# Opening of a first attention: doubled keys counted apart, maxima between the value block's tiles, values taken in two halves, last queries rounded later

## What is computed

```python
def attention_mixer(h, w_qkv, q_g, k_g, w_o, rope):   # 16 query heads, 4 key/value heads, head width 64
    qkv = h @ w_qkv
    q, k, v = jnp.split(qkv, [1024, 1280], axis=-1)
    q = rmsnorm(q.reshape(B, S, 16, 64), q_g)
    k = rmsnorm(k.reshape(B, S, 4, 64), k_g)
    v = v.reshape(B, S, 4, 64)
    q = axial_rope(q, rope)
    k = axial_rope(k, rope)
    # for each block of queries
    s = jnp.einsum('bqhgd,bkhd->bhgqk', qblk, k) * scale
    p = jax.nn.softmax(s, axis=-1)
    o = jnp.einsum('bhgqk,bkhd->bqhgd', p, v)
    return o @ w_o
```

## Time and profile before

| | |
|---|---|
| time, median of 3 runs | 1970.55 us (1969.24 to 1971.86) |
| time of the profiled execution | 1969.77 us |
| its span | 1968.0 us |
| TensorE busy | 1940.5 us, 99% of the span |
| VectorE, ScalarE, GpSimd busy | 1096.2, 751.2, 590.7 us |
| mean granted TensorE clock | 0.995 of full speed |

### The profile page before, as it was taken

How to read it: one execution, slowest core, us unless ns; L and a number is a source line. 1 busy time by engine, 2 the same in 40 slices (tenths; PEclk the granted TensorE clock), 3 DMA queues, 4 the chain that set the end, 5 groups by cost and what they waited for, 6 DMA issues and landing times.

```text
span 1968.0 us, 23603 instructions
## 1 busy us (share of the span) xinstructions
PE 1940.5 (99%) x9254; PEld 1601.6 (81%) x9254; DVE 1096.2 (56%) x1086; ACT 751.2 (38%) x838; POOL 590.7 (30%) x528
## 2 busy tenths in 40 slices
PE   9899999999999999999999999999999999999998
PEld 7655788888887988888888887889888888888886
DVE  6754355555557547455455557874344474545456
ACT  6456332222235534332232235455552353222223
POOL 1201279997000001289996002523210100000000
PEclk9999999999999999999999999999999999999999
DMA  6411244443322221144443233412133312323221
GB/s 230 108 10 22 86 150 171 152 159 111 107 86 97 92 102 43 65 167 154 171 149 123 86 106 113 118 43 74 55 107 107 107 51 78 107 85 107 87 105 64
DMA packets 42763, 204.51 MB, mean 104 GB/s; under 512 B 13248, under 2 KB 13376, under 8 KB 20160
## 3 DMA queue, kind: packets, MB, share of 16 engines
q1 hardware_dynamic: 34784, 167.82, 25.0%
q0 software_dynamic: 7904, 35.66, 6.0%
HBM read 190.84 MB, written 2.10 MB: 98 GB/s over the span
## 4 chain that ended last, share of the span: by engine, by line
PE 93%; DVE 3%; ACT 2%; issue 1%; DMA 0%; POOL 0%; SPq 0%; POOLq 0%; DVEq 0%; ACTq 0%
PE ps L261 24%; PE ps L263 24%; PE ps L262 24%; PE ps L693 3%; PE ps L2526 2%; PE ps L2528 2%; PE ps L2527 2%; PE ps L1738 1%; PE ps L293 1%; PE ps L292 1%; PE ps L291 1%; PE ps L680 1%; PE ps L661 1%; PE ps L679 1%; PE ps L1722 1%
## 5 line engine op out<-in xcount | busy, mean ns | idle before, releaser
L223 ACT ACTIVATE w_hi<-w_raw 128x2048 fp32r<-128x2048 f32 x141 | 270.3, 1917 | 713.3 <-PE ps L263 641.9
L231 DVE TENSOR_TENSOR w_lo<-w_raw,w_hi 128x2048 fp32r<-128x2048 f32 x139 | 323.1, 2324 | 112.8 <-ACT w_hi L223 110.7
L261 PE MATMUL ps<-h_hi,w_hi 128*128 128x512 f32 (+1 forms) x968 | 380.1, 393 | 4.2 <-DVE w_lo L231 3.1
L263 PE MATMUL ps<-h_hi,w_lo 128*128 128x512 f32 (+1 forms) x968 | 370.4, 383 | 0.0
L262 PE MATMUL ps<-h_lo,w_hi 128*128 128x512 f32 (+1 forms) x968 | 370.1, 382 | 0.0
L1510 POOL TENSOR_SCALAR ada_t<-ada_w,prm 128x256 f32<-128x256 f32 x192 | 220.4, 1148 | 13.0 <-DMA ada_w<-in_ada 12.1
L261 PEld LDWEIGHTS ps<-h_hi,w_hi 128*128 128x128 f32 x968 | 182.1, 188 | 42.3 <-issue 6.3
L263 PEld LDWEIGHTS ps<-h_hi,w_lo 128*128 128x128 f32 x968 | 181.8, 188 | 36.1
L262 PEld LDWEIGHTS ps<-h_lo,w_hi 128*128 128x128 f32 x968 | 182.2, 188 | 34.8 <-issue 1.7
L1032 DVE TENSOR_TENSOR x<-x,ps 128x1024 f32<-128x1024 f32 x128 | 155.6, 1216 | 79.8 <-PE ps L263 79.8
L261 PE MATMUL ps<-m_xhi,w_hi 128*128 128x512 f32 x512 | 200.0, 391 | 0.0
(11 more groups left out here) (360 smaller groups left out, 3076.7 us busy)
## 6 DMA issues: line engine op xcount, KB each, us to landing
w_raw<-in_wb SPq DMA_DIRECT2D x152, 1024.0 KB, 4.9
ada_w<-in_ada POOLq DMA_DIRECT2D x24, 1024.0 KB, 5.4
a_sw<-a_g POOLq DMA_DIRECT2D x20, 128.0 KB, 2.7
x<-in_xT SPq DMA_DIRECT2D x4, 512.0 KB, 7.0
ada_w<-ada_acc POOLq DMA_DIRECT2D x4, 384.0 KB, 5.2
out<-f_pad SPq DMA_DIRECT2D x3, 512.0 KB, 2.6
w_raw<-in_wb SPq DMA_DIRECT2D x4, 256.0 KB, 6.2
w_hi<-a_q POOLq DMA_DIRECT2D x4, 256.0 KB, 4.0
```

What stands on the lines that cost most here:

```text
L223: act.activation(w_hi[:, slot], w_raw[:, slot], ACT.Copy).then_inc(hi_done, 1)
L231: dve.tensor_tensor(w_lo[:, slot], w_raw[:, slot], w_hi[:, slot].bitcast(F32), ALU.subtract).then_inc(split_done, 1)
L261: pe.matmul(out, w[0], h[0], start=start, stop=False)
L263: return pe.matmul(out, w[1], h[0], start=False, stop=stop)
```

## The change

Five orders and counts are edited. No arithmetic is added or taken away.

- The transfers that double the keys now count up `a_moved[1]` and not `a_dup`. `maxima(0)` waits for 96 there (64 of `swap(1)` and 32 of the doubling), `scores(0)` waits for 64 in `a_dup` (`queries(1)` and `queries(2)`), `scores(16)` for 128. `sine(3)`'s count becomes 160. GpSimd gets two waits so that the counts can't be mixed.
- TensorE does `maxima(0)` after tile 0 of the value block, `aux(4)` and `maxima(1)` after tile 1, `maxima(2)` after tile 2 and `maxima(3)` after tile 3.
- VectorE's order for block 4 becomes `floor(4)`, `top(0)`, `low(3, 0)`, `low(3, 1)`, `cosine(4)`, `top(1)`, `sine(4)`, `rotated(4)`, `top(2)`, `rooted(4)`, `top(3)`. `low(4, r)` go to steps 2 and 4.
- ScalarE takes the values of tiles 0 and 1 once `aux(4)` is done, and those of tiles 2 and 3 after `probs(0)`. `values(0)` waits for the first half, `values(1)` for the second. `q_hi(4)` comes after `probs(1)`.
- GpSimd's `queries(3)` and `queries(4)` wait for the first scores and not for the end of block 5.

```diff
--- before.py
+++ after.py
@@ -651,7 +651,7 @@
                 h = p // 2
                 if p == 0:
                     pe.wait_ge(a_raw, 5)
-                    pe.wait_ge(a_dup, 96)
+                    pe.wait_ge(a_moved[1], 96)
                 else:
                     pe.wait_ge(a_top, p)
                 if p % 8 == 0:
@@ -666,12 +666,13 @@
                 h, pair = s // 2, 3 - s % 2
                 if s == 0:
                     pe.wait_ge(a_vset, 2)
+                    pe.wait_ge(a_dup, 64)
                 if s == 1:
                     pe.wait_ge(a_rs, 5)
                 if s >= 2:
                     pe.wait_ge(a_exp, s - 1)
                 if s == STEPS // 2:
-                    pe.wait_ge(a_dup, 160)
+                    pe.wait_ge(a_dup, 128)
                 if s % 2 == 0:
                     pe.wait_ge(a_row_in[h % 2], 64 * (h // 2 + 1))
                 for i in range(2):
@@ -683,8 +684,8 @@
             def values(s):
 
                 h = s // 2
-                if s == 0:
-                    pe.wait_ge(a_v_in, 2)
+                if s < 2:
+                    pe.wait_ge(a_v_in, s + 1)
                 if s % 2 == 0 and h >= 2:
                     pe.wait_ge(a_on, h - 1)
                 pe.wait_ge(a_exp, s + 1)
@@ -704,8 +705,12 @@
                 if j >= 2:
                     pe.wait_ge(a_raw, j - 1)
                 if j == V_BLOCK:
-                    pe_token_block(pe, b, b % 2, (j + 1) % 2, after=lambda t: aux(j - 1) if t == 0 else maxima(t - 1))
-                    maxima(2)
+                    def between(t):
+                        if t == 1:
+                            aux(V_BLOCK - 1)
+                        maxima(t)
+
+                    pe_token_block(pe, b, b % 2, (j + 1) % 2, after=between)
                     maxima(3)
                 elif j == 0:
                     pe_block(pe, b, b % 2, HH, (j + 1) % 2, rows=0)
@@ -751,14 +756,17 @@
                     dst = kv_heads("a_kh", r)[own[r]] if a == 0 else a_q2[own[r], 2 * a - 2:2 * a, r, :]
                     act.activation(dst, two(at_["a_rot"][own[r], a % 2]), ACT.Copy).then_inc(a_qhi, 1)
 
-            def take_v():
-                act.wait_ge(block_done, B_QKV + V_BLOCK + 1)
-                act.wait_ge(a_vset, 1)
-                act.wait_ge(n_std, 1)
-                for r in range(2):
-                    for t in range(TT):
+            def take_v(i):
+                if i == 0:
+                    act.wait_ge(a_aux, V_BLOCK)
+                    act.wait_ge(a_vset, 1)
+                    act.wait_ge(n_std, 1)
+                else:
+                    act.wait_ge(block_done, B_QKV + V_BLOCK + 1)
+                for t in (2 * i, 2 * i + 1):
+                    for r in range(2):
                         ins = act.activation(v_heads("a_v", r)[:, t], v_tokens(r)[:, t], ACT.Copy, scale=V_ROOT[:, t:t + 1])
-                    ins.then_inc(a_v_in, 1)
+                ins.then_inc(a_v_in, 1)
 
             for j in range(V_BLOCK):
                 evacuate(j)
@@ -769,7 +777,7 @@
                 if j == 0:
                     token_roots(act)
                 root(j)
-            q_hi(V_BLOCK - 1)
+            take_v(0)
 
             def probs(s):
                 act.wait_ge(a_S, s + 1)
@@ -795,7 +803,9 @@
                 if s < STEPS:
                     probs(s)
                 if s == 0:
-                    take_v()
+                    take_v(1)
+                if s == 1:
+                    q_hi(V_BLOCK - 1)
                 if s >= 3 and s % 2 == 1 and (s - 3) // 2 < HEADS:
                     inverse((s - 3) // 2)
                 if s >= 6 and s % 4 == 2 and (s - 6) // 4 < KT:
@@ -824,7 +834,7 @@
                 dve.tensor_tensor(two(at_["a_rot"][:, a % 2]), two(at_["a_g"][:, a % 2]), twice_row(at_["a_cos"][:]), ALU.mult)
 
             def sine(a):
-                dve.wait_ge(a_moved[a % 2], 64 * (a // 2 + 1))
+                dve.wait_ge(a_moved[a % 2], 160 if a == 3 else 64 * (a // 2 + 1))
                 sw = two(at_["a_sw"][:, a % 2])
                 link(dve, dve.tensor_tensor(sw, sw, twice_row(at_["a_sin"][:]), ALU.mult))
 
@@ -863,7 +873,7 @@
                 dve.tensor_tensor(at_["a_o"][own[r], t % 2, :], ps[own[r], r, :], at_["a_inv"][own[r]], ALU.mult).then_inc(a_on, 1)
 
             eps_row(dve)
-            for j in range(V_BLOCK):
+            for j in range(V_BLOCK - 1):
                 floor(j)
                 if j + 2 < N_QKV:
                     next_lo(dve, B_QKV + j + 2, (B_QKV + j) % 2)
@@ -871,20 +881,26 @@
                     for r in range(2):
                         low(j - 1, r)
                 cosine(j)
-                if j == V_BLOCK - 1:
-                    top(0)
                 sine(j)
-                if j == V_BLOCK - 1:
-                    top(1)
                 rotated(j)
                 rooted(j)
+            j = V_BLOCK - 1
+            floor(j)
+            top(0)
+            for r in range(2):
+                low(j - 1, r)
+            cosine(j)
+            top(1)
+            sine(j)
+            rotated(j)
             top(2)
+            rooted(j)
             top(3)
             for s in range(STEPS + 4):
                 if s + LEAD < STEPS:
                     top(s + LEAD)
-                if s < 2:
-                    low(V_BLOCK - 1, s)
+                if s in (2, 4):
+                    low(V_BLOCK - 1, s // 2 - 1)
                 if s >= 4 and s % 2 == 0 and (s - 4) // 2 < HEADS:
                     normed((s - 4) // 2)
                 if 22 <= s < 26:
@@ -916,15 +932,18 @@
             swap(0)
             swap(1)
             pool.wait_ge(a_ready, 1)
+            pool.wait_ge(a_moved[1], 64)
             for r in range(2):
                 kv = kv_heads("a_kh", r)
-                pool.dma_start(kv[own[1 - r]], kv[own[r]]).then_inc(a_dup, 16)
-            for a in range(2, V_BLOCK):
-                swap(a)
+                pool.dma_start(kv[own[1 - r]], kv[own[r]]).then_inc(a_moved[1], 16)
+            swap(2)
+            pool.wait_ge(a_moved[1], 96)
+            swap(3)
+            swap(4)
             pool.wait_ge(block_done, B_QKV + V_BLOCK)
             queries(1)
             queries(2)
-            pool.wait_ge(block_done, B_QKV + V_BLOCK + 1)
+            pool.wait_ge(a_S, 1)
             queries(3)
             queries(4)
             for t in range(KT):
```

## The result

The changed kernel takes 1960.03 us (median of 5 runs, 1958.75 to 1963.12) against 1970.55. The ratio is 0.9947 with a 95% interval of 0.9936 to 0.9958, that is 8.3 to 12.6 us less. The forecast was 1958.5 us, 12.0 less; the range of 1956.5 to 1963.3 holds the result. The median is near the edge of the forecast's own 1956.5 to 1960 and of rival 1's 1960.2 to 1963.6, so it is the profile, and not the time, that tells which of the two came. In the profiled execution the time is 1958.75 us (span 1957.0) against 1969.77 (1968.0).

The account below looks back on a forecast made before the run. TensorE, busy for 99% of the span, was taken as the bound. Idle gaps (5.4 us) plus clock and small joints (6.6) give 12.0 off 1969.77, or 1957.8; with the median 0.78 above, 1958.5 us, range 1956.5 to 1963.3.

Parts of the forecast that it names:

- rival 1: Clock falls once more behind the gaps left before `maxima(4)` and `maxima(5)`; 1960.2 to 1963.6 us, chance 0.32.
- The wait and its release: `maxima(0)` waits 3.53 us for queries' transfers it does not need; counted apart, it starts right behind tile 0.
- The timetable: Starts from tile 0 of the value block to `maxima(7)`, which moves from 110.58 to 98.55, 12.0 us sooner.
- The opening: Time from the start of the value block's tile 0 to the start of `maxima(7)`; 36.58 us before.
- The step that VectorE's chain just fits: Ten VectorE instructions of 1.23 us end at 89.05, in time for `top(3)` at 89.4 by 0.4 us.
- The sum by cause: Before `maxima(7)`, gaps of 7.7 us go and 2.25 stay or come, giving 5.4; clock and small joints give 6.6.
- The values: `take_v` in halves on ScalarE removes the 0.75 us gap before `values(0)`; the halves themselves cost nothing.
- The later rounding and the transfers: Moved `low(4, r)`, `q_hi(4)` and queries' transfers cost 0; bounds 1.2 us for rounding, 1 us for transfers.
- rivals 2 and 3: 2: only the first gap goes, 1965.3 us, chance 0.07; 3: the wait only moves to `scores(0)`, 1970.5 us, chance 0.03.
- The clock: The forecast's case: around the value block and first steps the clock does not fall again; chance 0.55.
- Rival 4: Clock falls in the first step and stays low while steps are filled; 1974.5 us, 4 us slower, chance 0.03.

Follow-up runs that it names:

- the second measurement: The changed kernel run once more with nothing edited, against the kernel before; 1959.53 us, ratio 0.9943.
- the last experiment: Changed kernel with a 128-column matmul behind each three of twelve two-column matmuls in the second modulation, four fewer in the next group; 1962.44 us, ratio 0.9960.

## Why the prediction was right, point by point

**The path.** The gain was to come from one wait, for transfers that `maxima(0)` did not need, from the chain behind it, and from the clock. The runs bear that out, with one part that was in some measure luck (the clock, below) and one that turned out small (VectorE's order).

**The wait and its release.** `maxima(0)` stood for the queries' transfers. With the count apart it starts behind tile 0 at once, and with the wait given back it stands for 9.07 us with the transfer named. Shown.

**The timetable.** The opening was to shrink from 36.58 to 24.55 us and measures 24.51, in four kernels within 0.01 us. Single starts are off by up to 0.2 us (`maxima(4)` at 90.53 for 90.7). The step that VectorE's chain just fits held: `rooted(4)` ends at 89.34, and `top(3)` waits 0.67 us for TensorE (0.4 was forecast). That no order gives the gain alone was not in the text, which summed by cause. The runs show how the parts lean on each other: the counting alone gives some 6 us, the orders without it none, VectorE's order without TensorE's nothing beyond the counting. TensorE's order without VectorE's gives nearly all: `top(0)` is 3.6 us later against tile 0, 0.9 of it is paid, and the median is within the spread of the changed kernel's. What must not be late is the end of VectorE's chain, as the forecast had it: with TensorE's old order `top(3)` starts 19.69 us behind tile 0's start against 15.25, and `maxima(4)` comes 4.43 us later, so the delay is paid in full.

**The sum by cause.** The forecast put 5.4 us on idle time and 6.6 on the clock and joints. By the profile's own column the gaps were 7.68 us and are 1.71, so 5.97 is idle time and 6.1 the rest. The forecast took the gaps before from that column and the gaps after as distances between starts, which are 0.16 us longer; the total is a distance between starts and does not hang on it. No run holds the clock up in the kernel before, so the clock's part is read from durations (`scores` takes 0.95 us at the full and 1.71 at the low clock) and is not tested by itself.

**The values.** The gap of 0.75 us went and the halves were hidden, as forecast. Mis-sized was "uncovered they would cost 1.1 us": it is 1.29 us of waiting, and in the profiled execution 3.1 us with the fall of the clock behind the third gap.

**The later rounding and the transfers** were taken at 0 and cost 0. The rounding gives 0 too. `scores(2)` had 0.6 us in hand by the forecast. Head 1's last small transfer goes out at about 93.1 and the slowest of the stage took 3.4 us, so it lands by 96.5 against 97.00. So neither VectorE's chain nor a row of maxima held the loop (rivals 2 and 3). The two kernels with a lead of three show what happens when that margin is spent.

**The clock.** The forecast's case, no fall, is what the profiles show: the pattern of 1.32 and 0.39 us stands in five profiled executions (the changed kernel twice, both halves late, rounding first, small matmuls broken up) and the clock fell in the opening in none of them. Nor did it with a lead of three (0.39 and 1.51 us). It fell in those with more or longer gaps: the counting alone, TensorE's old order, VectorE's old order, the values with one count, the lead of three with late transfers. But in the kernel that waits for the queries it fell behind 1.31 and 0.39 us as well, the very pattern that is left. So rival 1 named a real mechanism and the right two gaps; the pattern was followed by a fall in one profile of six and, in the changed kernel itself, in neither of two. The forecast's grounds against a fall, more matmuls between the two gaps and a shorter sum than before, hold in that kernel too. What differs there is the long wait with a low stretch of its own, over at 89.8 us, and no run shows whether it matters. That the clock stayed up was therefore in part luck. Whether the one run of 1963.12 us (clock 0.997) had such a fall has no trace to tell; its time lies where rival 1 put it. Rival 4, a clock that stays low, did not come.

**The missing 1.5 us** (12.0 forecast, 10.5 between the medians, 11.2 in the second measurement) is inside the interval. The forecast took the whole span to follow the opening. In the first profiles of the two kernels the opening gives 12.07 us, the value block starts 0.75 us later and what follows `maxima(7)` takes 0.32 us longer (1857.74 against 1857.42), which leaves the 11.0 us between the spans. Two things were seen that can make the rest. The value block starts anywhere from 73.86 to 74.75 us in the profiles. And the fall near 1172 us costs 1.7 us in most executions that have it and 3.4 in one (six of thirteen profiled ones have it, the last experiment left out). Whether that fall is more frequent than in the kernel before stays open: its single profile has none, and its other runs, at 0.993 to 0.997, can't be split between the two stages.

## What to carry to other kernels

Don't count transfers that are needed early with others that are issued later: the wait is for the last of them, the profile may name no engine for it, and moving the waiter forward only made it wait longer here (9.07 us for 3.53). In a stage where two engines alternate, write the timetable of both out: here its end held to 0.1 us. Then try the orders one by one: all together they gave nothing without the counting; with it, VectorE's gave nothing without TensorE's, and TensorE's gave nearly all without VectorE's. A gap of about 1 us beside others should be costed with the fall of the clock that it may bring: 1.29 us became 3.1 in one profile here. And a profile that kept the clock over such gaps does not show that the next execution will.

## What the hardware showed that I had not expected

The clock can fall near 1172 us with no idle gap before it. TensorE is busy for 2.00 of 2.00 us in the window ahead of the fall, but with 24 records of two columns each, and the eight records behind them take 5.38 us instead of 3.68. The same instructions kept the clock in seven of the thirteen profiles, so they do not decide it alone. The Trainium skill (TensorE: Matmul & The Clock Gate, Terms) says that a monitor of how busy TensorE is gates the clock. The trace agrees where a gap of 3.53 us stood ahead of the fall; here a full busy share in the profile did not keep the clock up. The attempt to break that group up did not settle why.

Small transfers of 0.5 KB on SyncE's queue take 2.0 us to land alone. Beside 256 KB transfers on GpSimd's queue they took 3.1 to 3.9 us with a lead of three, and up to 5.4 us with the late transfers, where `scores(4)` waited 2.46 us for them.
